# HGRN2's levels 32 and up one point later, and VectorE's takes and reciprocals in another order, in a fused decoder block

## The chip, the core and the metric

One NeuronCore of a Trainium2 chip runs the whole kernel. The metric is the device time of one execution in microseconds. Five engines run their own instruction streams and meet only at semaphores: TensorE (PE), VectorE (DVE), ScalarE (ACT), GpSimd (POOL) and SyncE (SP), which issues DMAs.

## What is computed

A decoder block on 1024 tokens of width 1024: a norm, one wide input projection, two branches with 8 heads of 128 each, an output projection, a final norm. Everything is float32.

```python
proj = jnp.einsum('bsd,de->bse', rmsnorm(x, norm_g), w_in)       # 1024 x 10240
sb_q, sb_k, sb_v, sb_z, hg_q, hg_f, hg_i, hg_z, gate_logits = jnp.split(proj, ...)
# branch 1, each query row: w = exp(log_sigmoid(z) + suffix sum of log_sigmoid(-z)); o = w @ v
# branch 2 (HGRN2), each head, in chunks:
S_t = diag(f_t) S_{t-1} + (1 - f_t) v_t^T ;  o_t = S_t^T silu(q_t)
hg_o = rmsnorm(hg_o, hg_norm_g)
u_sb = (sb_o * silu(sb_z)) @ w_sb_proj ;  u_hg = (hg_o * silu(hg_z)) @ w_hg_proj
y = sigmoid(gates[0]) * u_sb + sigmoid(gates[1]) * u_hg
out = rmsnorm(x + y @ w_out, final_norm_g)
```

## The kernel before

**Projections.** Columns of `w_in` are taken in pairs of 128 (a "pair", number n: four to a head, then eight "gate pairs"). A pair is a 2x2 block product done in Strassen's way with seven products in the order P1, P6, P7, P5, P2, P3, P4. A product is 12 matmuls of 128x512 (each operand is split into a high and a low part, and three of the four part products are taken). Six matmuls are a **point**, u: a pair has 14, half a head's work 28. ACT makes the high part of the seven weight operands (`split`, tile `b_hi`), POOL the sums and the low parts (`b_sum`, `t`, `b_lo`), always for the pair after the one that PE multiplies. DVE joins products out of PSUM into the four result blocks (`take_u2`, `take_u3`, `take_c22`, `take_c12`, `take_c21`). A product may overwrite its bank only when DVE has taken what stands there: P3 (points 10, 11 of a pair) waits for `take_c22` of the same pair.

**The loop.** PE's stream is written out by hand: `first_half` has the pairs q/k and v/z of head h, with the HGRN2 pieces of head h-1 between the points as `HG_AT` {point: piece} says; `second_half` has the pairs of HGRN2's inputs, with branch 1 of head h between the points (`QK_AT`, `TURN_AT`, `PV_AT`). Before the loop stands `second_half(0)`, after it the gate pairs, the first two with the last head's HGRN2 pieces. The loop runs seven times.

**HGRN2 pieces.** Pieces 3 to 7 are score matmuls of block sizes 4 to 64; before each, DVE multiplies `hq` and `hk` by decays (`grow`, L1341 to L1343). Piece 6 is size 32 (PE line L1807, 32 matmuls), 7 is size 64, 8 turns `hk`, 9 makes the chunk states' products, 11 the output, 12 the mean of squares for the norm. Between 9 and 11 DVE chains the states (`carry_states`), between 11 and 12 ACT squares the output and DVE makes its low part (`take_output`, tile `sq_lo`). After 12 ACT takes square roots and DVE inverts them in four quarters (`invert(a, 0..3)`, RECIPROCAL, L1450) and multiplies (`normalize`).

**Branch 1 on DVE.** In `second_half` each of eight query tiles j gets a pair of scans (`weigh(h, j)`: L1308 for its own 128 keys, L1313 for the keys before), and PE then turns the result (L1763).

**The start.** Before `second_half(0)` PE waits for four operand sums of the activations (`s_ready` 4), the last of which DVE makes at 64 to 66 us.

**Gate pairs.** Beside the takes DVE multiplies branch 1's stored outputs with their gates (`osb_multiply`, `osb_gate`, `osb_low`, tiles `osb_*`), ACT makes sigmoids and high parts (`osb_sigmoid`, `osb_high`) in its one stream with `split`.

Of the kernel before, what the change touches and what calls it, by code (L numbers as in the profile page):

```python
# [42 lines left out]
P1, P6, P7, P5, P2, P3, P4 = range(7)  # L43
# [12 lines left out]

SPLITS_BEFORE = {s: max(SPLIT_ORDER.index(t) for t in range(s + 1)) + 1 for s in range(PRODUCTS)}
# [21 lines left out]
HG_AT = {1: 0, 3: 1, 6: 3, 9: 4, 12: 5, 14: 6, 17: 7, 19: 8, 21: 9, 23: 11, 26: 12}  # L79
# [58 lines left out]
def build(nc, x, norm_g, w_in, b_gate, lb_logits, hg_norm_g, w_sb, w_hg, w_out, final_g, out):  # L138
    ctx = ExitStack()
    with ctx:  # L140
# [590 lines left out]
        def _(act):  # L731
# [183 lines left out]
            def sigmoids(h, j):  # L915
                n = (j + 1) * P
                act.wait_ge(qk_done, 8 * h + j + 1)
                bank, n_banks, m = score_banks(j)
# [148 lines left out]
            for g in range(N_GATE_PAIRS):  # L1067
# [3 lines left out]
                for p in range(PAIR_POINTS):  # L1071
# [31 lines left out]
                    if p == 7 and not final:  # L1103
                        for e in OSB_GATED.get(g, ()):
                            osb_high(e)
# [66 lines left out]
        def _(dve):  # L1172
# [284 lines left out]
            def first_half(h, n, pairs, attend):  # L1457

                a = h - 1
# [23 lines left out]
                take_u3(parts[1], n + 1)  # L1483
                if qk:
                    q_low(h)
                if attend:
                    carry_states(a)
                take_c22(pairs[1], n + 1, h)
                if attend:
                    take_output(a)  # L1490
                take_c12(pairs[1], n + 1)
                if attend:
                    invert(a, 0)
# [3 lines left out]
                if attend:  # L1497
                    invert(a, 1)
                    invert(a, 2)

            def second_half(h, attended_before):
# [4 lines left out]
                if attended_before:  # L1506
                    invert(h - 1, 3)
                    normalize(h - 1)
                weigh(h, 2)
                take_u3(QF_PAIR, n)  # L1510
# [76 lines left out]
            carry_states(a)  # L1587
            dve.wait_ge(gate_stored[1], 16)
            take_c22(GATE_PAIR, n)
            take_output(a)  # L1590
            take_c12(GATE_PAIR, n)
            for i in range(3):
                invert(a, i)
            dve.wait_ge(gate_stored[0], 16)
            take_c21(GATE_PAIR, n)
            invert(a, 3)
            normalize(a)
            for g in range(2, N_GATE_PAIRS):
# [3 lines left out]
                for e in OSB_GATED.get(g, ())[:1 if last_pair else None]:  # L1602
                    osb_gate(e)
# [8 lines left out]
                for e in OSB_GATED.get(g, ())[:1 if last_pair else None]:  # L1612
                    osb_low(e)
# [5 lines left out]
                if last_pair:  # L1619
                    for e in OSB_GATED[g][1:]:  # L1620
                        osb_gate(e)
                    for e in OSB_GATED[g][1:]:
                        osb_low(e)
# [54 lines left out]
        def _(pe):  # L1678
# [42 lines left out]
            def project(parity, n, p):  # L1721

                s = p // 2
                if p % 2 == 0:
                    product_waits(n, s)
                last = multiply(pair_bank(parity, s), s, range(2 * (p % 2), 2 * (p % 2) + 2), s <= P5)
# [243 lines left out]
            pe.wait_ge(s_ready, 4)  # L1970
# [92 lines left out]
```

## Time and profile before

| | us |
|---|---|
| median of 3 runs | 1359.86 (1359.74 to 1361.36) |
| the profiled execution, whole | 1358.94 |
| its span, first to last instruction | 1357.2 |
| PE busy | 1329.0 |
| DVE / POOL / ACT busy | 903.1 / 709.5 / 549.4 |

The span is what the profiler shows from the first to the last instruction; 1.7 us lie around it. Rows of the timeline give the start in us, the busy time in us, engine, line, operation, output and inputs, how many instructions are merged, and in square brackets how long the engine sat idle before and whom it waited for. A matmul's duration is latency: the next one starts about 0.23 us later.

### The profile page before, as it was taken

What the parts mean: (1) busy time and instruction counts of PE and PEld (TensorE: products, weight loads), DVE (VectorE), ACT (ScalarE), POOL (GpSimd) and SP (SyncE); (2) the same over time, 40 slices, a digit from 0 to 9 for tenths busy, and PEclk for the clock granted to TensorE, in tenths of its full rate; (3) what the DMA queues carried; (4) which work ended last, traced back from release to release, by engine and by line L of the source; (5) the groups of instructions that cost most, each with busy time, mean ns of one, the idle gap of its engine ahead of it and who ended that gap; (6) DMA issues with size and microseconds to landing.
All of it is one profiled execution on the core that took longest, in us unless ns stands there. A gap on an engine that the chain in (4) does not pass through costs nothing.

```text
span 1357.2 us, 22985 instructions
## 1 busy us (share of the span) xinstructions
PE 1329.0 (98%) x8393; PEld 1108.9 (82%) x8393; DVE 903.1 (67%) x1076; ACT 549.4 (40%) x899; POOL 709.5 (52%) x475
## 2 busy tenths in 40 slices
PE   8899999999999999999999999999999999999998
PEld 6788788788878878878888887887887888888886
DVE  5838877877877887787687788778635455645223
ACT  7543355255345335524534533552444431111121
POOL 5655564654665556455466556645578722223310
PEclk9999999999999999999999999999999999999999
DMA  5122111211112211121111211113543485434502
GB/s 187 31 62 65 47 62 32 82 58 46 62 46 73 66 32 62 31 92 56 37 62 46 77 62 31 62 31 118 176 180 133 155 266 191 124 93 132 202 27 98
DMA packets 128168, 118.55 MB, mean 87 GB/s; under 512 B 3920, under 2 KB 110464, under 8 KB 128128
## 3 DMA queue, kind: packets, MB, share of 16 engines
q1 hardware_dynamic: 118816, 92.81, 21.5%
q10 hardware_dynamic: 9312, 25.19, 5.4%
q8 instruction: 26, 0.43, 0.1%
q14 instruction: 14, 0.11, 0.0%
HBM read 88.63 MB, written 29.36 MB: 87 GB/s over the span
## 4 chain that ended last, share of the span: by engine, by line
PE 82%; DVE 7%; issue 5%; POOL 2%; ACT 2%; DMA 1%; ACTq 0%; DVEq 0%; SPq 0%; POOLq 0%
PE banks L1693 44%; PE banks L1986 13%; PE banks L2030 7%; PE banks L1773 5%; PE banks L1751 4%; PE banks L1763 2%; DVE hk L1176 2%; DVE forget L1176 2%; DVE scT L1422 1%; PE banks L1832 1%; PE banks L1737 1%; PE banks L1807 1%; POOL b_lo L631 1%; POOL b_sum L631 1%; PE banks L1834 1%
## 5 line engine op out<-in xcount | busy, mean ns | idle before, releaser
L1693 PE MATMUL banks<-a_hi,b_hi 128*128 128x512 f32 x1064 | 432.7, 407 | 6.4 <-issue 3.8
L1693 PE MATMUL banks<-a_hi,b_lo 128*128 128x512 f32 x1064 | 417.1, 392 | 0.0
L1693 PE MATMUL banks<-a_lo,b_hi 128*128 128x512 f32 x1064 | 415.7, 391 | 0.0
L631 POOL TENSOR_TENSOR b_lo<-w_raw,b_hi 128x512 fp32r<-128x512 f32 x106 | 162.2, 1540 | 231.9 <-ACT b_hi L733 231.9
L631 POOL TENSOR_TENSOR b_lo<-b_sum,b_hi 128x512 fp32r<-128x512 f32 x114 | 167.7, 1471 | 148.2 <-ACT b_hi L733 148.2
L1693 PEld LDWEIGHTS banks<-a_hi,b_hi 128*128 128x128 f32 x1064 | 200.3, 188 | 46.1 <-issue 7.5
L1693 PEld LDWEIGHTS banks<-a_hi,b_lo 128*128 128x128 f32 x1064 | 199.9, 188 | 44.3
L1693 PEld LDWEIGHTS banks<-a_lo,b_hi 128*128 128x128 f32 x1064 | 200.8, 189 | 35.9
L733 ACT ACTIVATE b_hi<-b_sum 128x512 fp32r<-128x512 f32 x114 | 72.0, 632 | 152.5 <-POOL b_sum L631 151.9
L717 POOL TENSOR_TENSOR w_lo<-w_raw,w_hi 128x1024 fp32r<-128x1024 f32 x20 | 54.5, 2730 | 133.5 <-ACT w_hi L733 133.5
L631 POOL TENSOR_TENSOR b_sum<-w_raw 128x512 f32<-128x512 f32 x68 | 102.9, 1513 | 0.0
L912 ACT ACTIVATE wT<-banks 128x512 f32<-128x512 f32 (+2 forms) x96 | 47.1, 491 | 109.5 <-PE banks L1763 93.8
L1313 DVE TENSOR_TENSOR_SCAN kappa<-kappa 128x128 f32<-128x128 f32 (+6 forms) x56 | 83.8, 1496 | 2.0
L1308 DVE TENSOR_TENSOR_SCAN kappa<-kappa,spared 128x128 f32<-128x128 f32 x64 | 44.0, 696 | 58.2 <-ACT kappa L925 58.2
L1773 PEld LDWEIGHTS banks<-wT,v_tok 128*128 128x128 f32 x576 | 74.1, 191 | 5.2
L1176 DVE TENSOR_TENSOR hq<-hq,forget 128x512 f32<-128x512 f32 (+1 forms) x64 | 65.8, 1029 | 17.5 <-PE banks L1807 15.1
L1176 DVE TENSOR_TENSOR u<-banks,u 128x512 f32<-128x512 f32 x76 | 51.6, 678 | 38.3 <-ACT u L733 30.2
L733 ACT ACTIVATE w_hi<-w_raw 128x1024 fp32r<-128x1024 f32 x20 | 21.0, 1059 | 134.1 <-DVE y_sum L1176 83.9
L1773 PE MATMUL banks<-wT,v_tok 128*128 128x128 f32 x576 | 74.5, 274 | 0.0
L733 ACT ACTIVATE b_hi<-t 128x512 fp32r<-128x512 f32 x38 | 24.0, 632 | 124.4 <-POOL t L631 124.4
L631 POOL TENSOR_TENSOR b_lo<-t,b_hi 128x512 fp32r<-128x512 f32 x38 | 56.8, 1494 | 31.0 <-ACT b_hi L733 31.0
L1176 DVE TENSOR_TENSOR hk<-hk,forget 128x512 f32<-128x512 f32 x56 | 67.7, 1209 | 0.0
(219 smaller groups left out, 2564.8 us busy)
## 6 DMA issues: line engine op xcount, KB each, us to landing
w_raw<-in_w_in SPq DMA_DIRECT2D x72, 512.0 KB, 4.9
gate_d<-gate_out SPq DMA_DIRECT2D x16, 512.0 KB, 4.6
gate_in<-gate_d ACTq DMA_DIRECT2D x32, 256.0 KB, 2.7
x_tok<-in_x SPq DMA_DIRECT2D x8, 512.0 KB, 6.6
z_d<-z_out SPq DMA_DIRECT2D x8, 512.0 KB, 2.7
hz_d<-z_out SPq DMA_DIRECT2D x8, 512.0 KB, 2.7
osb_d<-o_sb SPq DMA_DIRECT2D x8, 512.0 KB, 5.7
ohg_d<-hq SPq DMA_DIRECT2D x8, 512.0 KB, 2.7
```

The costliest lines, as they stand in the source:

```text
L631: return nc.gpsimd.tensor_tensor(dst, a, b, op)
L717: nc.gpsimd.tensor_tensor(lo, w_raw[:, t % 2, :, :], hi.bitcast(F32), ALU.subtract).then_inc(panel_ready, 1)
L733: return nc.scalar.activation(dst, src, ACT.Copy)
L912: nc.scalar.activation(wT[:, first:first + n, :].rearrange("p t e -> p (t e)"), turned[:, 0:n * P], ACT.Identity, scale=-1.0, bias=1.0).th ...
L1176: return v.tensor_tensor(dst, a, b, op)
L1308: last = v.tensor_tensor_scan(own, own, spared[:, ::-1], 1.0, ALU.mult, ALU.max)
L1313: last = v.tensor_tensor_scan(others, others, others, kappa[j % 2][:, S - P:S - P + 1], ALU.mult, ALU.min)
L1693: last = mm(bank, w[:, s, k, :], t[s][:, k, :], start=opens and k == 0 and z == 0, stop=k == QUAD - 1 and z == 2, skip_group_check=not opens)
L1751: last = mm(banks[:, bank + c, 0:m], tile(q, j), k[:, c * m:(c + 1) * m], start=z == 0, stop=z == 2)
L1773: last = mm(tile(attended, j % 4), v_tok[:, i, :], wT[:, i, :], start=i == 0, stop=i == j)
L1986: last = mm(pj[b], w[:, c, k, :], halfs(o[k], b), start=k == 0 and z == 0, stop=k == KT - 1 and z == 2, skip_group_check=True)
L2030: last = mm(dst, tile(y[k], i), w[:, first:first + n, k, :], start=k == 0 and z == 0, stop=k == KT - 1 and z == 2)
```

## The change

Pieces 6, 7, 8, 9, 11 and 12 of HGRN2 are put one point later in all engines' streams (`HG_AT`). In ACT's stream the weight splits of a point stand ahead of the piece of the same point, so the P1 split now stands ahead of piece 8's copies and the P5 split ahead of piece 11's squares. In DVE's stream `take_c22` of the second pair goes ahead of `carry_states`, `q_low` behind it, `take_c12` ahead of `take_output`, `take_c21` ahead of `invert(a, 0)`; of the four reciprocals two now stand behind `differences`, one behind `take_u2` of the next half and one, with `normalize`, behind `take_u3`. At the start PE's one wait for the four sums becomes a wait at each product that uses one, and ACT's second sigmoid waits for all four. In the gate pairs the second of two gate multiplications goes behind `take_c22`, its high part from p = 7 to p = 10.

```diff
-HG_AT = {1: 0, 3: 1, 6: 3, 9: 4, 12: 5, 14: 6, 17: 7, 19: 8, 21: 9, 23: 11, 26: 12}
+HG_AT = {1: 0, 3: 1, 6: 3, 9: 4, 12: 5, 15: 6, 18: 7, 20: 8, 22: 9, 24: 11, 27: 12}
+SUM_OPERANDS = (P7, P6, P5, P3)
...
             def sigmoids(h, j):
                 act.wait_ge(qk_done, 8 * h + j + 1)
+                if isinstance(h, int) and h == 0 and j == 1:
+                    act.wait_ge(s_ready, 4)
...
-                    if p == 7 and not final:
-                        for e in OSB_GATED.get(g, ()):
+                    if p in (7, 10) and not final:
+                        for e in OSB_GATED.get(g, ())[:1] if p == 7 else OSB_GATED.get(g, ())[1:]:
                             osb_high(e)
...
                 take_u3(parts[1], n + 1)
+                take_c22(pairs[1], n + 1, h)
+                if attend:
+                    carry_states(a)
                 if qk:
                     q_low(h)
-                if attend:
-                    carry_states(a)
-                take_c22(pairs[1], n + 1, h)
+                take_c12(pairs[1], n + 1)
                 if attend:
                     take_output(a)
-                take_c12(pairs[1], n + 1)
-                if attend:
-                    invert(a, 0)
                 take_c21(pairs[1], n + 1, h)
                 if qk:
                     differences(h)
                 if attend:
+                    invert(a, 0)
                     invert(a, 1)
-                    invert(a, 2)
...
                 take_u2(QF_PAIR, n)
                 if attended_before:
+                    invert(h - 1, 2)
+                weigh(h, 2)
+                take_u3(QF_PAIR, n)
+                if attended_before:
                     invert(h - 1, 3)
                     normalize(h - 1)
-                weigh(h, 2)
-                take_u3(QF_PAIR, n)
                 weigh(h, 3)
...
             take_u3(n, n)
-            carry_states(a)
             dve.wait_ge(gate_stored[1], 16)
             take_c22(GATE_PAIR, n)
+            carry_states(a)
+            take_c12(GATE_PAIR, n)
             take_output(a)
-            take_c12(GATE_PAIR, n)
-            for i in range(3):
-                invert(a, i)
             dve.wait_ge(gate_stored[0], 16)
             take_c21(GATE_PAIR, n)
-            invert(a, 3)
-            normalize(a)
+            invert(a, 0)
+            invert(a, 1)
             for g in range(2, N_GATE_PAIRS):
                 take_u2(n, n)
-                for e in OSB_GATED.get(g, ())[:1 if last_pair else None]:
+                if g == 2:
+                    invert(a, 2)
+                    invert(a, 3)
+                    normalize(a)
+                for e in OSB_GATED.get(g, ())[:1]:
                     osb_gate(e)
                 take_u3(n, n)
...
                     for e in OSB_TIMES_Z[g][1:]:
                         osb_multiply(e)
-                for e in OSB_GATED.get(g, ())[:1 if last_pair else None]:
+                    for e in OSB_GATED.get(g, ())[1:]:
+                        osb_gate(e)
+                for e in OSB_GATED.get(g, ())[:1]:
                     osb_low(e)
...
                 if p % 2 == 0:
                     product_waits(n, s)
+                    if isinstance(n, int) and n == 2 and s in SUM_OPERANDS:
+                        pe.wait_ge(s_ready, max(SUM_OPERANDS.index(t) for t in SUM_OPERANDS if t <= s) + 1)
...
-            pe.wait_ge(s_ready, 4)
             pe.wait_ge(const_made, CONSTANTS)
             second_half(0)
```

PE's stream in `first_half`, from the last matmuls of point 14 to the first of point 16 (the second pair's P1 has `a_*_49`, P6 `a_*_50`; L1807, after the change L1819, is piece 6). Before:

```order
L1693 MATMUL banks<-a_hi_49,b_hi 128x512
L1693 MATMUL banks<-a_lo_56,b_hi 128x512
L1693 MATMUL banks<-a_hi_49,b_lo 128x512
L1798 REGISTER_ALU
L1799 REGISTER_ALU
L1807 MATMUL banks<-hq,hk 32x32 x16
L1693 MATMUL banks<-a_hi_49,b_hi 128x512
```

After:

```order
L1702 MATMUL banks<-a_hi_49,b_lo 128x512
L1810 REGISTER_ALU
L1811 REGISTER_ALU
L1819 MATMUL banks<-hq,hk 32x32 x16
L1710 REGISTER_ALU
L1702 MATMUL banks<-a_hi_50,b_hi 128x512
```

The six matmuls of point 15 have gone from behind the piece to ahead of it.

DVE's stream near the end of `first_half`: the third take of the second pair (`z_out<-banks,u_78`, `take_c12`) and `take_output` (`sq_lo`, then `hq<-banks`). Before, from the second take (`take_c22`) on:

```order
L1176 TENSOR_TENSOR z_out<-banks,u_79 128x512
L1443 ISA
L1176 TENSOR_TENSOR sq_lo<-scT,sq_hi 128x512
L1443 REGISTER_ALU
L1176 TENSOR_TENSOR sq_lo<-scT,sq_hi 128x512
L1446 ISA
L1446 TENSOR_SCALAR hq<-banks,small 128x512 x2
L1252 REGISTER_ALU
L1254 REGISTER_ALU
L1176 TENSOR_TENSOR z_out<-banks,u_78 128x512
```

After:

```order
L1181 TENSOR_TENSOR q_lo<-q_raw,q_hi 128x1024
L1257 REGISTER_ALU
L1259 REGISTER_ALU
L1181 TENSOR_TENSOR z_out<-banks,u_78 128x512
L1448 ISA
L1181 TENSOR_TENSOR sq_lo<-scT,sq_hi 128x512
L1448 REGISTER_ALU
L1181 TENSOR_TENSOR sq_lo<-scT,sq_hi 128x512
L1451 ISA
L1451 TENSOR_SCALAR hq<-banks,small 128x512 x2
```

`take_c12` has gone from behind `take_output` to ahead of it, and `q_low`, further up before, stands here.

DVE's stream in `second_half`, from `take_u2` (`u_78<-banks,u_79`) to `take_u3` (`u_79<-banks,u_78`) and what follows it. Before (L1450 is the reciprocal, L1308 and L1313 the scans of tile 2, then of tile 3):

```order
L1176 TENSOR_TENSOR u_78<-banks,u_79 128x512
L1450 RECIPROCAL scT<-scT 128x256
L1176 TENSOR_TENSOR hq<-hq,scT 128x1024
L1305 REGISTER_ALU
L1308 SCALAR_TENSOR_TENSOR kappa_95<-kappa_95,spared 128x128
L1311 REGISTER_ALU
L1313 SCALAR_TENSOR_TENSOR kappa_95<-kappa_95 128x256
L1252 REGISTER_ALU
L1254 ISA
L1176 TENSOR_TENSOR u_79<-banks,u_78 128x512
L1305 REGISTER_ALU
L1308 SCALAR_TENSOR_TENSOR kappa_96<-kappa_96,spared 128x128
```

After (L1455 the reciprocal, L1313 and L1318 the scans):

```order
L1181 TENSOR_TENSOR u_78<-banks,u_79 128x512
L1455 RECIPROCAL scT<-scT 128x256
L1310 REGISTER_ALU
L1313 SCALAR_TENSOR_TENSOR kappa_95<-kappa_95,spared 128x128
L1316 REGISTER_ALU
L1318 SCALAR_TENSOR_TENSOR kappa_95<-kappa_95 128x256
L1257 REGISTER_ALU
L1259 ISA
L1181 TENSOR_TENSOR u_79<-banks,u_78 128x512
L1455 RECIPROCAL scT<-scT 128x256
L1181 TENSOR_TENSOR hq<-hq,scT 128x1024
L1310 REGISTER_ALU
```

One reciprocal stands behind `take_u2` as before, now without `normalize` behind it; another, with `normalize`, stands behind `take_u3`. Between tile 0's scans and `take_c22` there are two reciprocals where there was one.

## Rows read from the trace of the kernel before

**Rows 1.** Waits of the whole trace, PE: releaser, total us, times, longest.

```profile
PE banks L1807 <- DVE hk L1176: 10.3, 8, 1.3
PE banks L1693 <- issue: 3.8, 1, 3.8
PE banks L1693 <- DVE gate_out L1176: 2.6, 2, 2.2
```

**Rows 2.** Stretches: length, then each engine's busy us, PE's clock, DMA.

```profile
66.70:71.50 4.80, 4.76 (x16) 3.91 (x17) 0.99 (x1) 1.18 (x3) 4.06 (x4) 0.64 0.30 115
264.90:377.58 112.68, 111.37 (x803) 93.47 (x802) 85.96 (x104) 50.11 (x84) 65.13 (x45) 1.00 0.18 56
300.18:312.33 12.15, 12.15 (x64) 10.34 (x62) 12.01 (x13) 4.34 (x9) 7.31 (x5) 1.00 0.11 44
```

**Rows 3.** Timeline, DVE and PE at piece 6 in the loop's second round.

```profile
264.90 1.76 DVE L1176 TENSOR_TENSOR hk<-hk,forget 128x512 f32<-128x512 f32 x1
266.79 0.70 PE L1807 MATMUL banks<-hq,hk 128*32 128x32 f32 x32 [1.31 <-DVE hk L1176]
```

**Rows 4.** Timeline of the start, PE, ACT and DVE.

```profile
66.74 0.67 PE L1693 MATMUL banks<-a_hi,b_hi 128*128 128x512 f32 x1 [3.76 <-issue]
76.87 0.27 PE L1763 MATMUL banks<-ident,kappa 128*128 128x128 f32 x1
70.16 0.63 ACT L733 ACTIVATE b_hi<-b_sum 128x512 fp32r<-128x512 f32 x1 [2.91 <-POOL b_sum L631]
71.70 0.60 ACT L733 ACTIVATE u<-banks 128x512 f32<-128x512 f32 x1 [0.90 <-PE banks L1693]
73.55 0.42 DVE L1308 TENSOR_TENSOR_SCAN kappa<-kappa,spared 128x128 f32<-128x128 f32 x1 [5.85 <-ACT kappa L925]
```

**Rows 5.** Timeline, DVE and PE, a second half inside the loop.

```profile
300.18 0.74 DVE L1308 TENSOR_TENSOR_SCAN kappa<-kappa,spared 128x128 f32<-128x128 f32 x2 [0.19 <-ACT kappa L925]
301.93 1.74 DVE L1450 RECIPROCAL scT<-scT 128x256 f32<-128x256 f32 x1
304.85 1.51 DVE L1308 TENSOR_TENSOR_SCAN kappa<-kappa,spared 128x128 f32<-128x128 f32 x1
306.40 1.60 DVE L1313 TENSOR_TENSOR_SCAN kappa<-kappa 128x256 f32<-128x256 f32 x1
311.67 0.66 DVE L1176 TENSOR_TENSOR forget<-banks,u 128x512 f32<-128x512 f32 x1
312.50 0.39 PE L1693 MATMUL banks<-a_hi,b_hi 128*128 128x512 f32 x1
```

**Rows 6.** Timeline, POOL in the same second half, then DVE in round 0's.

```profile
304.12 1.96 POOL L631 TENSOR_TENSOR b_lo<-w_raw,b_hi 128x512 fp32r<-128x512 f32 x1 [6.33 <-ACT b_hi L733]
78.68 0.75 DVE L1313 TENSOR_TENSOR_SCAN kappa<-kappa 128x256 f32<-128x256 f32 x1
```

**Rows 7.** Timeline: PE at point 24, POOL's next low part, a near tie elsewhere.

```profile
288.27 0.39 PE L1693 MATMUL banks<-a_hi,b_lo 128*128 128x512 f32 x1
289.98 1.29 POOL L631 TENSOR_TENSOR b_lo<-b_sum,b_hi 128x512 fp32r<-128x512 f32 x1 [1.86 <-ACT b_hi L733]
273.59 1.85 POOL L631 TENSOR_TENSOR b_lo<-b_sum,b_hi 128x512 fp32r<-128x512 f32 x1 [5.80 <-ACT b_hi L733]
273.61 0.69 DVE L1176 TENSOR_TENSOR hk<-hk,forget 128x512 f32<-128x512 f32 x1
```

**Rows 8.** Timeline of the gate pairs, DVE, ACT and PE.

```profile
969.57 4.97 DVE L1450 RECIPROCAL scT<-scT 128x256 f32<-128x256 f32 x3 [1.44 <-ACT scT L956]
971.34 1.15 ACT L1036 ACTIVATE gate_out<-gate_out,small 128x1024 f32<-128x1024 f32 x1
975.13 0.72 ACT L1036 ACTIVATE gate_out<-gate_out,small 128x512 f32<-128x512 f32 x1 [2.63 <-DVE gate_out L1176]
1023.73 0.47 PE L1693 MATMUL banks<-a_hi,b_hi 128*128 128x512 f32 x1 [2.21 <-DVE gate_out L1176]
1062.50 0.47 PE L1693 MATMUL banks<-a_hi,b_hi 128*128 128x512 f32 x1 [0.41 <-DVE gate_out L1176]
```

More of the change, by code:

```diff
@@ L1621, in _ @@
                         osb_gate(e)
-                    for e in OSB_GATED[g][1:]:
-                        osb_low(e)
+                for e in OSB_GATED.get(g, ())[1:]:
+                    osb_low(e)
                 dve.wait_ge(gate_stored[0], 16 * g)
```

## The prediction

> **What bounds the kernel now.** Read the table of stretches first. One round of the loop is 112.68 us and PE is busy for 111.37 of it, at the full clock [rows 2]. So TensorE bounds the kernel, and only an edit that fills a hole in PE's stream can gain. The list of waits has all holes that are not in the first 30 us: 10.3 us in 8 waits for `hk`, one of 3.8 us with no releaser named, and 2.6 us in two waits for `gate_out` [rows 1]. The timeline gives their places: the `hk` wait is piece 6, 1.31 us each round [rows 3]; the 3.8 us is the start of `second_half(0)` [rows 4]; the two others are in gate pairs 4 and 6 [rows 8]. Together 16.7 us, the most that this change can bring but for the clock. The second question is what is nearly late now. DVE is busy for 12.01 of the 12.15 us between tile 0's scans and the end of `take_c22` [rows 2], and PE's P3, which waits for that take, starts at 312.50, while the take ends at 311.67 + 0.66 = 312.33 [rows 5]. DVE's results reach PE 0.13 us after their end (264.90 + 1.76 = 266.66, PE goes at 266.79 [rows 3]), so the margin there is 312.50 - 312.46 = 0.04 us.
>
> **The start.** PE idles 3.76 us and then starts at half clock: the 4.80 us behind it have a mean clock of 0.64 [rows 2, 4], which costs 0.36 x 4.80 = 1.7 us. The new waits are all met when PE comes: P1 needs no sum, the others are made by DVE before. PE alone would reach tile 0's turn, now at 76.87, 3.76 + 1.7 = 5.5 us earlier, at 71.4. But the turn needs DVE's scan, that needs ACT's sigmoid, and this stands in ACT's stream behind the P4 split, which waits for POOL and runs from 70.16 to 70.79 whatever PE does [rows 4]. Behind it come the copy of P1 (now 71.70, held 0.90 by PE), tokens, sigmoid. The scan starts 1.85 after that copy (73.55 - 71.70). New: 70.8 + 1.85 = 72.65, scan done 73.07, PE 73.2. The gain is 76.87 - 73.2 = **3.7 us**, and PE's new idle time of 1.8 us is shorter than the 2.21 in gate pair 4; that row's next matmul takes 0.47 against the 0.67 after the 3.76 [rows 4, 8], so I expect no half clock. If it came nevertheless, 1.7 less.
>
> **Piece 6 in the loop, seven times.** PE now runs point 15 (six matmuls at 0.23, 1.37 us) ahead of the piece. It was free 1.31 us before `hk`; the point fills this, and the piece and all pieces behind it start when they did, with one point more done. Each later piece keeps its distance to the one before, so what stands between them is as early as now. `take_c22` ahead of `carry_states` costs nothing, since DVE waits for piece 9 there anyway. Removed: **1.31 us a round**, 9.2 in seven.
>
> **What the next half pays.** The second half starts 1.37 us earlier than the HGRN2 pieces. Ahead of `take_c22` there is now one reciprocal more: 4.97 / 3 = 1.66 us [rows 8]. The margin is 0.04, so if DVE's stretch only grew by this, P3 would wait 1.6 us. But part of the stretch is not work. Tile 2's scans take 1.51 and 1.60 us [rows 5], where the same forms take 0.42 and 0.75 in round 0 [rows 4, 6]: 1.94 us of waiting, and beside them POOL's low part takes 1.96 [rows 6] instead of the 1.29 that it takes alone [rows 7]. An operation of DVE with two SBUF inputs and one of POOL never run together there. The reciprocal has one input and doesn't wait (1.74 with POOL idle [rows 5], 1.66 in a row of three with POOL at work [rows 8]). With `normalize` gone from ahead of tile 2's scans, do they miss POOL's operation? Their own scan comes 1.75 + 1.66 = 3.41 us after tile 0's (301.93 - 300.18, plus the reciprocal), the other 0.46 later, at 3.87; POOL's comes at 304.12 - 300.18 = 3.94. So the two are almost tied. Scans first: 1.94 saved, 1.66 paid, P3 waits 0. POOL first: only the own scan is freed (1.51 - 0.42 = 1.09 saved), 1.66 paid, and `normalize`, now beside POOL's next operations, can wait another 0.3 to 1: P3 waits 0.9 to 1.6. All of it against us: 1.66 + 1.29 (one POOL operation more) = 2.95. I take **0.9 us a round**, about midway between the two cases, since a second thing works against DVE: between the halves POOL's T4 sum no longer finds P4 the last to come, so `differences` falls beside POOL's operations, and behind it the P4 split and tile 0's sigmoid can come a little late, which turns the near tie towards POOL. Bounds 0 and 2.95.
>
> The Trainium skill, SBUF — State Buffer, section Who interferes with whom, has this as a rule: a DVE instruction with two SBUF inputs and a GpSimd instruction that reads SBUF exclude each other, and the one that issues first holds the shared port for its whole length. The trace agrees in the 1.51, 1.60 and 1.96 us above. In one place it does not to the letter: POOL's row starts at 273.59 and DVE's at 273.61, and DVE runs its 0.69 undisturbed while POOL takes 1.85 [rows 7]; row starts tell the order to no better than some hundredths.
>
> **A second tie, ahead of piece 12.** `take_c12`, due one point after piece 11, now stands ahead of `take_output`. Point 25's last matmul will start where point 24's does, 288.27, so the take starts at 288.27 + 0.39 + 0.13 = 288.8, the two `sq_lo` at 289.4 and 290.0 (0.69 each as `hk` in the same form, less 0.08 by which such rows overlap), where POOL's next low part starts at 289.98 [rows 7]. If POOL wins, `sq_lo` ends at 289.98 + 1.29 + 0.5 = 291.8, 0.7 us late for piece 12. By the row of the near tie DVE wins; I take 0 and keep 0.7 as a rival.
>
> **Gate pairs.** The eighth `hk` wait, 1.25 of the 10.3 us, goes as in the loop. The 2.21 us before P3 of pair 4 are DVE doing two gate multiplications ahead of `take_u3`; the second one is moved. But removing a hole here only helps if the later take is not late too, and pair 6 still has 0.41 [rows 8]: ACT's and POOL's chain of splits is as late as PE there. What moves that chain is the other edit: ACT waits 2.63 us at 975.13 for a `take_c21` that stands behind three reciprocals of 4.97 us [rows 8], and these are now behind it; also the 1.15 us sigmoid at 971.34 comes ahead of the square roots. So the chain starts 2.6 to 3.8 us earlier, less 0.3 for the high part moved to p = 10. PE's holes would give 1.25 + 2.21 + 0.41 = 3.9. I take **3.2 us**, bounds 2.3 and 3.9. The 270 us behind the gate pairs have no hole that this touches.
>
> **Sum.** -3.7 - 7 x (1.31 - 0.9) - 3.2 = -3.7 - 2.9 - 3.2 = -9.8 us. The profiled execution took 1358.94, 0.92 less than the median; from the median 1359.86 it is **1350.0 us**. A difference of 0.2% (2.7 us) is about what a measurement of this kernel can tell from none.
>
> **Rivals.**
> *All of it stays*: tile 2's scans slip in ahead of POOL and P3 never waits. For it speaks 3.87 against 3.94, against it the late sigmoid. -3.7 - 9.2 - 3.3 = -16.2: 1343.7.
> *`sq_lo` behind POOL*: 0.7 a round lost at piece 12; the second half then has 0.7 more room and P3 waits 0 to 0.2. -3.7 - 7 x 0.55 - 3.3 = -10.9: 1349. By the skill's rule as written (first to issue holds the port) POOL's 289.98 ahead of 290.0 would give just this.
> *Paid back in full*: P3 waits 1.3 to 1.6 a round; the loop gives 0 to +2, start and gates stay: -5 to -7, 1353 to 1355.
> *Slower*: tile 2's scan, `normalize` and tile 3's scans each fall in behind one POOL operation and P3 waits up to 2.95: the loop costs 7 x (2.95 - 1.31) = +11.5, in all +4.6: 1364.5. It decides from a P3 wait of 2.3 on (7 x (2.3 - 1.31) = 7 uses up start and gates). For it speaks that POOL and DVE alternate where both have work; against it that one POOL operation more would have to be met, with POOL busy 7.31 of the 12.15 us [rows 2].
> *The change doesn't do what it says* (piece 6 still waits): the point is 1.37 and the hole 1.31, so at most 0.1 us remains; 2 in 100.
>
> **How the numbers follow.** Forecast 0.42, all stays 0.20, `sq_lo` behind POOL 0.13, paid back in full 0.13, slower or close to it 0.12. Faster by over 0.2%: 0.42 + 0.20 + 0.13 + most of the fourth = 0.80 after rounding down for what I overlooked; slower 0.09, same 0.11. The range takes in the clean case with gates at 3.9 (1343) and the paid-back case up to a P3 wait of 2.0: 1342.5 to 1357.5.
>
> **What the profile will show.** Right: no wait for `hk` at piece 6; 8 waits fewer; start hole of about 1.8 instead of 3.76, at tile 0's turn, clock 1.00 behind it; a round of 112.3; a PE wait of about 0.9 before P3 of the third pair, released by `forget<-banks`; no 2.21 in gate pair 4. Wrong: a round of 111.4 (the tie falls to DVE), a new PE wait ahead of the mean of squares (piece 12), released by `sq_lo` (the second tie), or a round over 112.7 (POOL and DVE alternate through the stretch).

## The result: 0.68% slower, and where the time went

| | before | after |
|---|---|---|
| median | 1359.80 (1358.45 to 1361.36, 4 runs) | 1369.05 (1367.56 to 1370.49, 4 runs) |
| the profiled execution, whole | 1358.94 | 1367.56 |
| its span | 1357.2 | 1365.8 |
| PE / DVE busy | 1329.0 / 903.1 | 1336.4 / 934.9 |

The ratio is 1.0068, with an interval of 1.0050 to 1.0085. Forecast were 1350.0 and a range up to 1357.5, so the direction was wrong and the time outside the range. In the experiments below one of the ten executions of extra_recip took 2210.12 us at a mean clock of 0.556, and its figures leave that one out.

PE's waits after the change, from the list of waits of the whole trace (releaser, total us, times, longest), to be held against [rows 1]:

```profile
PE banks L1702 <- DVE forget L1181: 12.5, 7, 1.8
PE banks L1851 <- DVE sq_lo L1181: 2.8, 6, 0.5
PE banks L1775 <- DVE kappa L1313: 1.6, 1, 1.6
PE banks L1702 <- DVE gate_out L1181: 1.6, 3, 0.8
```

The wait for `hk` is gone, all eight times. Two waits that before did not have are there instead: P3's for `take_c22` (`forget`), seven times 1.79 us, and piece 12's for `sq_lo`, 0.47 in most rounds. In the timeline of PE, after the change, a round looks like this; the third line is the new idle time at the start, where [rows 4] had 3.76:

```profile
289.24 0.50 PE L1851 MATMUL banks<-sq_hi,mean_w 128*128 128x512 f32 x1 [0.47 <-DVE sq_lo L1181]
310.97 0.52 PE L1702 MATMUL banks<-a_hi,b_hi 128*128 128x512 f32 x1 [1.79 <-DVE forget L1181]
...
72.98 0.33 PE L1775 MATMUL banks<-ident,kappa 128*128 128x128 f32 x1 [1.61 <-DVE kappa L1313]
```

The table of stretches of the changed kernel shows what a round costs (length, busy us of PE, its weight loads, DVE, ACT, POOL, then PE's clock and DMA). Two whole rounds, each from one P3 start to the next, and then the first 4 us behind two of these P3 starts:

```profile
197.10:310.97 113.87, 111.60 (x801) 93.52 (x802) 90.95 (x104) 49.78 (x85) 64.68 (x45) 1.00 0.18 56
310.97:426.46 115.49, 113.25 (x802) 94.84 (x802) 90.89 (x104) 49.78 (x85) 64.66 (x45) 0.99 0.18 54
...
197.00:201.10 4.10, 4.00 (x23) 3.51 (x24) 3.15 (x3) 1.52 (x3) 2.13 (x3) 1.00 0.00 0
310.90:315.00 4.10, 4.03 (x15) 3.51 (x16) 3.12 (x3) 0.37 (x1) 2.07 (x2) 0.58 0.00 0
```

A round took 112.68 before [rows 2]. Now it takes 113.9 at full clock, and 115.5 where TensorE's granted clock falls behind P3's wait (0.58 of full speed over the next 4 us, the lower of its two levels, 1.2 GHz, for most of them). Behind 4 of the 7 waits it did (310.97, 426.46, 542.00, 770.70), behind 3 it did not. The first matmuls after such a wait show the fall; the distance from start to start goes from 0.23 to 0.43 us:

```profile
427.02 0.40 PE L1702 MATMUL banks<-a_hi,b_lo 128*128 128x512 f32 x1
427.25 0.52 PE L1702 MATMUL banks<-a_hi,b_hi 128*128 128x512 f32 x1
427.57 0.63 PE L1702 MATMUL banks<-a_lo,b_hi 128*128 128x512 f32 x1
428.00 0.63 PE L1702 MATMUL banks<-a_hi,b_lo 128*128 128x512 f32 x1
```

Why P3 waits is in the timeline of DVE and POOL, after the change, in a second half of the loop (before: [rows 5], [rows 6]):

```profile
300.27 0.36 DVE L1313 TENSOR_TENSOR_SCAN kappa<-kappa,spared 128x128 f32<-128x128 f32 x1
300.66 1.83 DVE L1318 TENSOR_TENSOR_SCAN kappa<-kappa 128x256 f32<-128x256 f32 x1
302.42 0.66 DVE L1181 TENSOR_TENSOR u<-banks,u 128x512 f32<-128x512 f32 x1
303.00 1.74 DVE L1455 RECIPROCAL scT<-scT 128x256 f32<-128x256 f32 x1
304.77 2.23 DVE L1181 TENSOR_TENSOR hq<-hq,scT 128x1024 f32<-128x1024 f32 x1
306.93 1.51 DVE L1313 TENSOR_TENSOR_SCAN kappa<-kappa,spared 128x128 f32<-128x128 f32 x1
308.47 1.86 DVE L1318 TENSOR_TENSOR_SCAN kappa<-kappa 128x384 f32<-128x384 f32 x1
310.26 0.66 DVE L1181 TENSOR_TENSOR forget<-banks,u 128x512 f32<-128x512 f32 x1
...
300.66 1.29 POOL L633 TENSOR_TENSOR b_lo<-w_raw,b_hi 128x512 fp32r<-128x512 f32 x1 [6.84 <-ACT b_hi L735]
304.63 1.29 POOL L633 TENSOR_TENSOR b_lo<-b_sum,b_hi 128x512 fp32r<-128x512 f32 x1 [1.06 <-ACT b_hi L735]
305.88 2.28 POOL L633 TENSOR_TENSOR b_sum<-w_raw 128x512 f32<-128x512 f32 x1
```

Tile 2's own scan is free, 0.36 instead of 1.51. The other scan (tile 2's, of the keys before) and POOL's low part both have a row that starts at 300.66; POOL takes its 1.29 undisturbed and the scan 1.83 instead of 0.75. Then POOL's next low part starts 0.14 ahead of the norm's product, which takes 2.23 where [rows 5]'s kernel had 1.23 for it, and tile 3's own scan takes 1.51. The Trainium skill (SBUF — State Buffer, section Who interferes with whom) says that issue order and not the form of the operation decides who blocks; the 304.63 against 304.77 agrees with that, and at 300.66 the rows cannot tell the order.

The wait at piece 12 has the same cause. DVE and POOL, after the change, ahead of 289.24:

```profile
286.17 0.69 DVE L1181 TENSOR_TENSOR z_out<-banks,u 128x512 f32<-128x512 f32 x1 [3.13 <-PE banks L1702]
286.78 2.41 DVE L1181 TENSOR_TENSOR sq_lo<-scT,sq_hi 128x512 fp32r<-128x512 f32 x2
...
287.35 2.99 POOL L633 TENSOR_TENSOR b_lo<-w_raw,b_hi 128x512 fp32r<-128x512 f32 x2 [3.19 <-ACT b_hi L735]
```

The two `sq_lo` take 2.41 together (0.69 each where POOL is idle, below), and end at 289.19; PE goes at 289.24.

### The profile page after: what moved, and what is told of

It is laid out like the page before. It is cut to its first block, busy times and chain, and to the rows that moved or that the text cites. A ratio compares the mean times of both kernels' runs of the same rounds, so it can differ in the third digit from the quotient of the medians.

```text
span 1365.8 us, 22986 instructions
## 1 busy us (share of the span) xinstructions
PE 1336.4 (98%) x8393; PEld 1114.7 (82%) x8393; DVE 934.9 (68%) x1076; ACT 547.2 (40%) x899; POOL 708.5 (52%) x475
## 4 chain that ended last, share of the span: by engine, by line
PE 86%; DVE 5%; issue 4%; ACT 3%; POOL 1%; DMA 1%; DVEq 0%; SPq 0%; ACTq 0%; POOLq 0%
PE banks L1702 48%; PE banks L1997 13%; PE banks L2041 6%; PE banks L1785 5%; PE banks L1763 3%; PE banks L1775 2%; PE banks L1844 1%; DVE scT L1455 1%; PE banks L1825 1%; PE banks L1819 1%; PE banks L1846 1%; PE banks L1839 1%; PE banks L1749 1%; DVE kappa L1313 1%; DVE sq_lo L1181 1%
## 5 line engine op out<-in xcount | busy, mean ns | idle before, releaser
L633 POOL TENSOR_TENSOR b_lo<-w_raw,b_hi 128x512 fp32r<-128x512 f32 x106 | 157.1, 1492 | 263.9 <-ACT b_hi L735 262.9
L633 POOL TENSOR_TENSOR b_sum<-w_raw 128x512 f32<-128x512 f32 x68 | 109.7, 1614 | 0.0
L1318 DVE TENSOR_TENSOR_SCAN kappa<-kappa 128x128 f32<-128x128 f32 (+6 forms) x56 | 91.1, 1626 | 2.0
L1181 DVE TENSOR_TENSOR hq<-hq,forget 128x512 f32<-128x512 f32 (+1 forms) x64 | 73.6, 1150 | 17.7 <-PE banks L1819 15.3
L1313 DVE TENSOR_TENSOR_SCAN kappa<-kappa,spared 128x128 f32<-128x128 f32 x64 | 39.6, 627 | 59.5 <-ACT kappa L930 59.4
L633 POOL TENSOR_TENSOR b_lo<-t,b_hi 128x512 fp32r<-128x512 f32 x38 | 52.7, 1386 | 31.0 <-ACT b_hi L735 31.0
L735 ACT ACTIVATE b_hi<-w_raw 128x512 fp32r<-128x512 f32 x106 | 64.5, 628 | 4.9 <-DMA w_raw<-in_w_in 3.6
```

The source lines that it names most:

```text
L633: return nc.gpsimd.tensor_tensor(dst, a, b, op)
L735: return nc.scalar.activation(dst, src, ACT.Copy)
L1181: return v.tensor_tensor(dst, a, b, op)
L1313: last = v.tensor_tensor_scan(own, own, spared[:, ::-1], 1.0, ALU.mult, ALU.max)
L1318: last = v.tensor_tensor_scan(others, others, others, kappa[j % 2][:, S - P:S - P + 1], ALU.mult, ALU.min)
```

## The experiments

Ten kernels. Where a median of before stands beside one, it was measured on the same chip at the same time.

### start_only: the kernel before with the start of the changed one

```diff
+                if isinstance(h, int) and h == 0 and j == 1:
+                    act.wait_ge(s_ready, 4)
...
+                    if isinstance(n, int) and n == 2 and s in SUM_OPERANDS:
+                        pe.wait_ge(s_ready, max(SUM_OPERANDS.index(t) for t in SUM_OPERANDS if t <= s) + 1)
...
-            pe.wait_ge(s_ready, 4)
```

> The kernel before with the change's first part alone: PE waits for each activation sum at the product that uses it, ACT's second sigmoid waits for all four. Everything else is as before. Expected: the start hole of 3.8 us and the half clock behind it go, a hole of about 1.6 us stands ahead of the first tile's turn, the rest of the trace is shifted and no more. 3.7 to 3.9 us faster, 1356. A rival theory, that the start's gain is lost again by the weights of pair 3 coming late, gives 0 to 3.

Measured: 1355.41 (1354.41 to 1356.32), before 1359.17; ratio 0.9970 (0.9959 to 0.9982). That is 3.8 us, and the wait at tile 0's turn is 1.65 at 73.74. The start does what was forecast, and the loss lies elsewhere.

### c22_ahead: the changed kernel, `take_c22` ahead of tile 3's scans

```diff
-                weigh(h, 3)
                 take_c22(QF_PAIR, n, h)
+                weigh(h, 3)
                 weigh(h, 4)
```

> The changed kernel with one swap: DVE takes c22 of the third pair ahead of tile 3's scans instead of behind them. Theory 1 (P3's 1.79 us wait and the half clock that follows it in five or six rounds of seven are all of the loss): the take is done about 3.3 us earlier, the wait is gone, no clock drop, a round is 112.69 - 1.31 + 0.47 = 111.85, and the time is about 1369.1 - 7 x 1.8 - 6 x 1.6 = 1347. Theory 2 (DVE as such is the bound in this half): the wait moves on to tile 3's turn, 1 us or more, and the time is over 1357.

Measured: 1347.16 (1345.28 to 1347.44), ratio 0.9906 (0.9889 to 0.9922). One swap of two lines turns 9.2 us more than before into 12.0 us less, each against its own measurement of before. P3's wait is gone, and the lower clock with it (mean clock 0.999, 0.994 in the changed kernel). The expectation's 1347 was met in part by luck: it counted 1.8 for each wait and six falls of the clock, 22.2 in all, where the profile has 4 falls and a wait costs 2.09 (below), 21.0 in all. The swap doesn't say why the take was late: it moves more work out of its way than P3 waited. A round is 111.85, of which piece 12's wait is left:

```profile
287.28 0.50 PE L1851 MATMUL banks<-sq_hi,mean_w 128*128 128x512 f32 x1 [0.47 <-DVE sq_lo L1181]
```

### recips_back: the changed kernel with the reciprocals where they were

```diff
                 if attend:
                     take_output(a)
+                    invert(a, 0)
                 take_c21(pairs[1], n + 1, h)
                 if qk:
                     differences(h)
                 if attend:
-                    invert(a, 0)
                     invert(a, 1)
+                    invert(a, 2)
...
-                if attended_before:
-                    invert(h - 1, 2)
-                weigh(h, 2)
-                take_u3(QF_PAIR, n)
                 if attended_before:
                     invert(h - 1, 3)
                     normalize(h - 1)
+                weigh(h, 2)
+                take_u3(QF_PAIR, n)
```

> The changed kernel with the four reciprocals and the product behind them where they stood before (one ahead of the second pair's c21, two behind differences, one with the product behind u2 of the next half). If the second reciprocal among the scans is the cause, P3's wait falls by 1.66 or more. But the reciprocals now wait for square roots one point later, so differences and tile 0's scans come late: I expect PE to wait up to 1.5 us for differences ahead of the token turn, and P3 0.5 to 1.5 us. A round of 113 to 114.5, 1360 to 1368.

Measured: 1359.33 (1358.51 to 1360.42), ratio 0.9999 (0.9989 to 1.0009). P3's wait is gone here too, but the reciprocal that is back ahead of `take_c21` and `differences` makes these late, and PE waits for `v_diff` ahead of a turn, 1.36 to 1.39 us in five rounds and 2.22 in two:

```profile
407.92 1.09 PE L1748 MATMUL banks<-ident,v_diff 128*128 128x128 f32 x8 [1.38 <-DVE v_diff L1329]
```

A round takes 113.5, which is 9.7 us less in all than the changed kernel and 12.2 more than c22_ahead. The late place of the reciprocals is thus not the fault by itself: with one swap behind it (c22_ahead), it is the better place. The old place together with that swap was not tried.

### output_ahead: the changed kernel, `take_output` ahead of `take_c12`

```diff
-                take_c12(pairs[1], n + 1)
                 if attend:
                     take_output(a)
+                take_c12(pairs[1], n + 1)
```

> The changed kernel with the low parts of the squares ahead of the c12 take, as before the change. Theory: the 0.47 us wait ahead of the mean of squares is POOL's operation between the two low parts; with the take behind them they are done 0.6 us earlier and this wait goes. The second half then starts 0.5 us earlier and P3's wait grows by up to the same, so the sum stays: 1367 to 1370. If P3's wait does not grow, 7 x 0.5 = 3.3 us less, 1365.8.

Measured: 1360.34 (1358.49 to 1362.30), ratio 1.0006 (0.9996 to 1.0016): 8.7 less than the changed kernel, a larger gain than either expectation had. Piece 12's wait is gone and P3's is 1.79 as in the changed kernel. The table of stretches shows two kinds of round again:

```profile
311.88:425.06 113.18, 111.39 (x801) 93.55 (x801) 90.58 (x104) 49.78 (x85) 64.26 (x45) 1.00 0.18 56
538.24:653.04 114.80, 113.01 (x801) 95.00 (x801) 90.59 (x104) 49.77 (x85) 64.25 (x45) 0.99 0.18 55
```

At full clock a round is 0.7 shorter (113.18 against 113.87), 4.2 in six rounds. The rest is clock: here the level fell behind 2 of the 7 P3 waits, there behind 4, at 1.6 us each 3.2 between these two profiles, whose spans differ by 1365.8 - 1359.1 = 6.7. The two come to 7.4, and 0.7 goes off again, because the turn of tile 0 comes at 73.68 in this profile and at 72.98 in the other. 8.7 is between the medians, for which other runs can have had other falls.

### c22_and_output_ahead: both swaps

> Both swaps at once: c22 of the third pair ahead of tile 3's scans, and the low parts of the squares ahead of the c12 take. Each alone took away its own wait (1.79 us and 0.47 us a round) and nothing came in its place. Expected: no PE wait left in the loop, a round of 112.69 - 1.31 = 111.38, 7 x 0.47 = 3.3 us less than with the first swap alone, 1343.9. Rival: the 0.5 us earlier start of the second half makes another take late, and the time stays at 1347.

Measured: **1342.44** (1342.07 to 1342.93), before 1360.28, ratio 0.9873 (0.9856 to 0.9889), the fastest of all. The profile has no PE wait left in the loop. With `take_output` first, the two `sq_lo` run at 0.69 each (timeline of DVE, this kernel), and piece 12 starts 111.1 us after the one of the round before:

```profile
282.91 0.69 DVE L1181 TENSOR_TENSOR sq_lo<-scT,sq_hi 128x512 fp32r<-128x512 f32 x1 [2.80 <-ACT sq_hi L957]
...
285.73 0.40 PE L1851 MATMUL banks<-sq_hi,mean_w 128*128 128x512 f32 x1
396.82 0.40 PE L1851 MATMUL banks<-sq_hi,mean_w 128*128 128x512 f32 x1
```

It was 1.5 faster than expected. The reason is a term that was missing in all sums up to here, the prediction's too. A round without a wait takes 396.82 - 285.73 = 111.09. With the one wait of 0.47 it takes 111.85, so that wait costs 0.76; with P3's 1.79 alone it takes 113.18, which is 2.09 more; and the round before, with 1.31 [rows 3], took 112.68, which is 1.59 more. A PE wait costs the idle time shown and 0.3 us (0.28 to 0.30). Of this 0.17 is how idle time is counted, from the end of the last matmul (its row is 0.40 long), while without a wait the next one would have started 0.23 after its start. Another 0.11 lies behind the wait: the first matmul starts 0.34 ahead of the second (289.24 and 289.58 in the changed kernel) and not 0.23 (285.73 and 285.96 here).

### recip_out: the changed kernel with one reciprocal left out

The reciprocal behind `take_u2` is left out, so one quarter of the norm's factors is not inverted and the output is not the block's. The next reciprocal counts for two at the semaphore.

```diff
...
-                if attended_before:
-                    invert(h - 1, 2)
                 weigh(h, 2)
                 take_u3(QF_PAIR, n)
                 if attended_before:
-                    invert(h - 1, 3)
+                    invert(h - 1, 3, 2)
```

> The changed kernel without the third reciprocal (the one behind u2), seven times: a quarter of HGRN2's norm is then not inverted, so that the output isn't the reference's; nothing else is left out. Additive theory (DVE's work ahead of c22 grew by one reciprocal of 1.66 us, that is the wait): P3's wait falls from 1.79 to about 0.1. Sequence theory (tile 2's scans can't start before ACT's sigmoid anyway, at 3.4 us after tile 0's, so that this reciprocal stands in idle time, and it is the reciprocal and the product behind u3 that push tile 3's scans behind POOL's operations): P3's wait stays at 1.8.

Measured: 1347.21 (1346.84 to 1347.93), ratio 0.9907 (0.9891 to 0.9924). P3's wait is gone. Timeline of DVE and POOL, this kernel:

```profile
297.80 0.42 DVE L1313 TENSOR_TENSOR_SCAN kappa<-kappa,spared 128x128 f32<-128x128 f32 x1 [1.40 <-ACT kappa L930]
298.26 0.75 DVE L1318 TENSOR_TENSOR_SCAN kappa<-kappa 128x256 f32<-128x256 f32 x1
301.28 1.22 DVE L1181 TENSOR_TENSOR hq<-hq,scT 128x1024 f32<-128x1024 f32 x1
...
298.36 1.73 POOL L633 TENSOR_TENSOR b_lo<-w_raw,b_hi 128x512 fp32r<-128x512 f32 x1 [6.83 <-ACT b_hi L735]
```

The tie goes the other way: the scan starts 0.10 ahead of POOL's operation and takes 0.75, POOL waits (1.73 instead of 1.29), and the product behind it is undisturbed. From tile 0's scans (294.55) to the end of `take_c22` it takes 11.87 us instead of 14.07 (11.47 in the loop's first round): 2.2 less for one reciprocal of 1.66, of which 1.40 is even spent in waiting for ACT. Tile 2's own scan starts only 0.17 earlier (3.25 behind tile 0's instead of 3.42), close to what I had expected, and this was enough to turn the tie. As for P3's wait, the additive theory's forecast (about 0.1) was the nearer one, and mine of 1.8 was wrong; as for the stretch, 2.2 is more than the 1.66 that were left out.

### product_behind: the changed kernel, the norm's product behind `take_c22`

```diff
                 if attended_before:
                     invert(h - 1, 3)
-                    normalize(h - 1)
                 weigh(h, 3)
                 take_c22(QF_PAIR, n, h)
+                if attended_before:
+                    normalize(h - 1)
```

> The changed kernel with the norm's product (hq by scT, 1.23 us alone, 2.23 in the trace) behind c22 instead of ahead of tile 3's scans. If POOL and DVE taking turns is what makes the wait, c22 comes about 2.1 us earlier, more than the 1.23 us of the product, and P3's wait is gone; additive theory: it falls by 1.23 to 0.56. The product is then 5 us later, and so is its store; ACT's copy into hq waits for that at point 9, which may cost PE 0 to 2 us elsewhere. 1347 to 1358.

Measured: 1347.84 (1347.51 to 1348.09), ratio 0.9911 (0.9894 to 0.9927). P3's wait is gone again, though the product moved out is work of only 1.22 us; counted as work, it would have left 0.56. Timeline of DVE, this kernel, where tile 3's own scan takes 0.35 instead of 1.51:

```profile
295.71 0.74 DVE L1313 TENSOR_TENSOR_SCAN kappa<-kappa,spared 128x128 f32<-128x128 f32 x2 [0.83 <-ACT kappa L930]
...
303.52 0.35 DVE L1313 TENSOR_TENSOR_SCAN kappa<-kappa,spared 128x128 f32<-128x128 f32 x1
303.92 1.87 DVE L1318 TENSOR_TENSOR_SCAN kappa<-kappa 128x384 f32<-128x384 f32 x1
305.70 0.66 DVE L1181 TENSOR_TENSOR forget<-banks,u 128x512 f32<-128x512 f32 x1
```

The stretch is 305.70 + 0.66 - 295.71 = 10.65, 3.4 less than the changed kernel's (in one round 11.42, where PE then waits 0.64 us for branch 1's `wT`).

### extra_recip: the kernel before with one reciprocal more

This is the sharpest one. It adds to the kernel before, behind the norm's product, a reciprocal of a tile that is written anew before its next use. Ahead of `take_c22` DVE then has the same operations as in the changed kernel, in another order.

```diff
                     normalize(h - 1)
+                    v.reciprocal(quarter(v_diff, 0), quarter(v_diff, 0))
                 weigh(h, 2)
```

> The kernel before with one more reciprocal of 128x256, on values that nobody needs, between the norm's product and tile 2's scans, seven times: the same work ahead of c22 as in the changed kernel, in another order. Additive theory: P3, with 0.04 us of margin, waits 1.6 us a round, 11 us slower and more where the clock falls. Sequence theory: the reciprocal has one input and runs beside POOL's operation, for which tile 2's first scan waits anyway (1.09 us), and the second scan then meets one less; P3 waits 0 to 0.3, the time is 1360 to 1362.

Measured: 1359.09 (1358.61 to 1361.38 in nine executions), before 1360.28, ratio 0.9995 (0.9985 to 1.0005): 1.66 us more work of DVE in every round, in a stretch in which DVE was busy for 12.01 of 12.15 us [rows 2], and no change of the time. The stretch is even as long as before (301.89 to 313.97, 12.08). Timeline of DVE, this kernel:

```profile
306.57 1.75 DVE L1509 RECIPROCAL v_diff<-v_diff 128x256 f32<-128x256 f32 x1
308.24 1.11 DVE L1308 TENSOR_TENSOR_SCAN kappa<-kappa,spared 128x128 f32<-128x128 f32 x1
309.38 0.75 DVE L1313 TENSOR_TENSOR_SCAN kappa<-kappa 128x256 f32<-128x256 f32 x1
...
313.31 0.66 DVE L1176 TENSOR_TENSOR forget<-banks,u 128x512 f32<-128x512 f32 x1
...
307.76 1.30 POOL L631 TENSOR_TENSOR b_sum<-w_raw 128x512 f32<-128x512 f32 x1
```

The reciprocal takes the place of waiting. POOL's sum runs its 1.30 beside it. All of these side by side, in one round each, the operations that differ (us of each row; tile 3's other scan, 1.85 to 1.87 in every kernel, is left out). Undisturbed are the scans of round 0 [rows 4, 6] and recip_out's product:

| kernel | stretch | tile 2 own | tile 2 other | product | tile 3 own | P3 waits |
|---|---|---|---|---|---|---|
| undisturbed | | 0.42 | 0.75 | 1.22 | 0.42 | |
| before | 12.15 | 1.51 | 1.60 | 1.23 | 1.35 | 0 |
| extra_recip | 12.08 | 1.11 | 0.75 | 1.23 | 0.87 | 0 |
| changed | 14.07 | 0.36 | 1.83 | 2.23 | 1.51 | 1.79 |
| recip_out | 11.87 | 0.42 | 0.75 | 1.22 | 1.51 | 0 |
| product_behind | 10.65 | 0.36 | 1.83 | (behind) | 0.35 | 0 |

Over the undisturbed times, the four operations lose 0 + 1.08 + 1.01 + 1.09 = 3.2 us in the changed kernel and 0.69 + 0 + 0 + 0.45 = 1.1 in extra_recip, with the same work. The difference of 2.1 is that of the stretches (14.07 - 12.08 = 2.0), and about what P3's wait costs (1.79 and 0.3 as above). So this wait is not the added reciprocal as an amount of work. It is how DVE's two-input operations fall against POOL's. That it is POOL which they wait for is read from the times of the rows; no kernel here moves POOL's operations.

### gates_back: c22_ahead with the gate multiplications as before

```diff
-                    if p in (7, 10) and not final:
-                        for e in OSB_GATED.get(g, ())[:1] if p == 7 else OSB_GATED.get(g, ())[1:]:
+                    if p == 7 and not final:
+                        for e in OSB_GATED.get(g, ()):
...
-                for e in OSB_GATED.get(g, ())[:1]:
+                for e in OSB_GATED.get(g, ())[:1 if last_pair else None]:
                     osb_gate(e)
...
-                    for e in OSB_GATED.get(g, ())[1:]:
-                        osb_gate(e)
...
```

The swap of c22_ahead is in it too, and the low parts (`osb_low`) follow the multiplications.

> The changed kernel with take_c22 ahead of tile 3's scans, and with the second gate multiplication and its high part where they stood before (behind take_u2 and at p = 7). Against c22_ahead (1347.2) this undoes one of the two edits in the gate pairs. Theory of the prediction: the 2.21 us hole ahead of P3 in pair 4 comes back (2.0 to 2.4), but the chain of splits is as late as PE in pairs 5 and 6, so that their holes (0.84 and 0.61) shrink or go: 0.8 us slower than c22_ahead, 1348.0, in bounds of 0.3 and 2.1. Rival (the hole alone decides): 2.1 slower, 1349.3, with 0.84 and 0.61 as they are. Second rival: the take order was the cause of all of the gates' gain and the reciprocals' place gave nothing: 2.9 slower, 1350.1.

Measured: 1347.02 (1345.18 to 1347.87), ratio 0.9904 (0.9887 to 0.9920). All three expectations were too high: it is c22_ahead's time (1347.16). The hole ahead of P3 in pair 4 comes back at 0.95 and not at 2.21. Timeline of PE at P3 of pairs 2, 4 and 6, this kernel; c22_ahead has 0.16, 0.84 and 0.61 in pairs 2, 5 and 6 instead (1.61 in all, here 1.55):

```profile
971.86 0.47 PE L1700 MATMUL banks<-a_hi,b_hi 128*128 128x512 f32 x1 [0.16 <-DVE gate_out L1181]
1011.13 0.47 PE L1700 MATMUL banks<-a_hi,b_hi 128*128 128x512 f32 x1 [0.95 <-DVE gate_out L1181]
1049.91 0.47 PE L1700 MATMUL banks<-a_hi,b_hi 128*128 128x512 f32 x1 [0.44 <-DVE gate_out L1181]
```

Moving the multiplication only moves idle time from one pair to another, as the prediction's argument on the chain of splits had it. What the change gains in the gate pairs comes from its other edits there, the takes ahead of the states and the reciprocals behind `take_c21`; which of these, and how much each, was not tried.

### before_c22: the kernel before, `take_c22` ahead of tile 3's scans

The same swap as in c22_ahead, made in the kernel before.

> The kernel before, with take_c22 of the third pair ahead of tile 3's scans, as the best version has it. There PE never waited for this take (margin 0.04 us), so the theory expects no change: 1359.9, within 0.7, piece 6's waits of 1.31 as before and P3's wait 0. Rival (the swap is a gain of its own, because DVE's stretch is full): up to 1.3 a round, 1350.8, if hk came earlier too. Second rival (tile 3's scans, now behind the take, are late for PE's turn of tile 3): a new wait for kappa, up to 1.5 us a round, 1370.

Measured: 1359.12 (1358.02 to 1361.27, 10 runs), before 1359.78; ratio 0.9997 (0.9987 to 1.0006). All seven waits for `hk` in the loop stand at 1.29 to 1.31, and no wait for `kappa` is new. The swap is worth nothing by itself; with the change it is worth 22 us.

## Why the prediction was wrong, point by point

**The start** was right: 3.7 forecast, 3.8 measured, with an idle time of 1.61 where 1.8 was forecast, no lower clock behind it, and the scan as what PE waits for.

**Piece 6** was right in kind and too small: the wait went as said, but removing 1.31 of idle time gives 1.59 a round, as worked out above. The other waits were priced too low in the same way.

**The second tie** fell to POOL. The prediction took 0 for it and priced the rival at 0.7 a round. The price was right (0.76), the choice wrong. The reading "DVE wins by the row of the near tie" took one undecidable pair of rows for a rule. The tie itself was there as forecast: undisturbed, the second `sq_lo` would have started 0.61 behind the first, at 287.39, and POOL's row starts at 287.35. In the one round without this wait the first starts at 633.33, the second would follow at 633.94, POOL's row starts at 633.91, and there the two `sq_lo` take 1.28 together: DVE won. Such rows tell a near tie, not its winner.

**The step that failed is P3's wait**, taken at 0.9 as "about midway between the two cases". The mechanism was the one described: the own scan freed (1.15 saved against 1.09), POOL first in the tie, 1.66 paid. Then the numbers left the sum. Tile 2's other scan grew by 0.23, tile 3's own by 0.16, and the product by the full 1.0 that stood as the upper end of "0.3 to 1". -1.15 + 0.23 + 1.0 + 0.16 + 1.66 = 1.9, which is 14.07 - 12.15, and P3 waited 1.79. The product goes with the first tie: where POOL won it, the product took 2.23 (changed, c22_ahead, output_ahead), where DVE won it, 1.22 (recip_out). So the two cases were two sequences, and a midway value described neither. That the sequence decides and not an amount is shown by two kernels above all: in extra_recip 1.66 us more work cost nothing, and in product_behind 1.22 us less ahead of the take shortened the stretch by 3.4. The margin was a little larger than the 0.04 of the prediction: PE goes 0.05 behind this take (310.26 + 0.66 = 310.92, then 310.97), not 0.13, which gives 0.12.

**The reciprocal** does run beside POOL, as the prediction had it, but the row of 4.97 us that it was read from had POOL at work for its first 2.1 us only (POOL's sum ends at 970.42 + 1.30 = 971.72). The 1.75 and 1.30 in extra_recip show it.

**No term for the clock** stood in the loop's sum. The prediction asked after the clock at the start alone, and took the 2.21 us in gate pair 4, behind which nothing fell in the profile of before, as a sign that a shorter gap is safe. In the three other kernels with a gap of 2.12 to 2.16 at that place it fell (last section). Behind 1.79 us it fell in 4 rounds of 7, at 1.6 us each.

**Gate pairs** gave less than forecast. c22_ahead gains 12.0 by the medians; less 3.8 for the start and 7 x (112.68 - 111.85) = 5.8 for the loop, this leaves 2.4, and by the spans of the profiles (1357.2 - 1345.7 = 11.5) 1.9. Forecast were 3.2, in bounds of 2.3 and 3.9. Of idle time 1.25, 2.21 and 0.41 went and 1.61 came in pairs 2, 5 and 6 (c22_ahead); the forecast left only 0.7 for such holes. That "removing a hole here only helps if the later take is not late too" was borne out by gates_back.

**The sum again**, by measured terms: -3.8 for the start, 7 x (113.87 - 112.68) = +8.3 for the rounds at full clock, less 0.8 for the one round in which piece 12 does not wait, 4 x 1.6 = +6.4 for the lower clock, -1.9 for the gate pairs, together +8.2. The two profiled executions differ by 1367.56 - 1358.94 = 8.6. Of the rivals "slower" came nearest in its sign. It set the point from which it decides at a P3 wait of 2.3; the measured wait was 1.79. Piece 12 (0.76 a round) and the clock made up what was missing, and neither was counted along with it; the 0.3 us of P3's wait cancels against that of the wait for `hk`. The cases were treated as if they excluded each other, while two ties falling to POOL have one cause and came together. Both of its signs of being wrong on that side appeared, the wait ahead of piece 12 and the round over 112.7.

**Open**: what makes the clock fall behind one gap and not behind an equal one. That the wait at piece 12 has a part in it is suggested by 4 of 6 rounds with it (changed) against 2 of 8 without (one of the changed kernel, seven of output_ahead), one profile each, which shows nothing firm.

## What to carry to other kernels

Where VectorE and GpSimd both have two-input work, price an edit by the sequence: write down which operation of the one meets which of the other, and follow the row of collisions to the take that TensorE waits for. Here one reciprocal more was free in one order (1359.09 against 1360.28), and one less was worth 22 us in another (1347.21 against 1369.05). Put the result that the bounding engine waits for ahead of work with slack before anything else is tuned. Price a new wait of TensorE at its idle time and 0.3 us, and give a stretch at the lower clock (1.6 us here, behind 4 of 7 gaps of 1.79 in one kernel and 2 of 7 in another) a chance of its own in the sum.

## What the runs showed of the hardware

**The clock falls behind equal gaps only sometimes.** The gap ahead of P3 in gate pair 4 has the same work around it in four kernels. In before (2.21 us, [rows 8]) the clock stayed at its full level. In before_c22 (2.12), start_only (2.16) and extra_recip (2.16) it fell, to 0.57 to 0.61 over the next 4 us. Two stretches, of before and of before_c22, right behind that gap (PE's clock is the third number from the end):

```profile
1023.60:1025.60 2.00, 1.87 (x8) 1.59 (x9) 2.00 (x2) 0.86 (x1) 2.00 (x2) 1.00 0.46 185
```

```profile
1022.80:1024.80 2.00, 1.94 (x5) 1.58 (x6) 2.00 (x2) 0.78 (x1) 2.00 (x2) 0.57 0.51 204
```

In recips_back gaps of 1.36 to 2.22 us, one in each of seven rounds, left the clock at 1.00 in the 4 to 5 us behind each.

**A reciprocal can be free in a stretch in which VectorE has no idle time.** In extra_recip it took 1.75 us, and the three scans that wait in before were 0.40, 0.85 and 0.48 shorter, 1.73 in all: it used time that two-input operations had spent waiting for GpSimd. Busy rows of VectorE hold such waits, and a busy share of 99% (12.01 of 12.15, [rows 2]) said nothing on how much room there was.
